# An attention stage of one core whose sparse blocks run in another order, large beside small, with the local blocks between them

## What is computed

```python
# sparse: per block of 128 queries, the 256 best keys by an indexer, 8 heads, one key/value head
score = jnp.where(causal[None], score, -jnp.inf)
_, sel = lax.top_k(score, topk)
logits = jnp.einsum('bqhd,bqkd->bhqk', qb, kg) * scale + bias
logits = jnp.where(valid[:, None], logits, -jnp.inf)
p = jax.nn.softmax(logits, axis=-1)
...
# local: window of 128, 8 query heads, 2 key/value heads, a learned sink per head
logits = jnp.where(mask, logits + bias, -jnp.inf)
m = jnp.maximum(jnp.max(logits, axis=-1, keepdims=True), sink)
p = jnp.exp(logits - m) / (jnp.sum(jnp.exp(logits - m), axis=-1, keepdims=True) + jnp.exp(sink - m))
```

## Time and profile before

| | before |
|---|---|
| three executions, us | 3624.54, 3630.03, 3897.19 |
| median, us | 3630.03 |
| the profiled execution, us | 3625.67 |
| its span in the profile, us | 3623.6 |
| TensorE busy, of the span | 3391.3 us (94%) |
| VectorE / ScalarE / GpSimd busy | 69% / 46% / 19% |

### The profile page before, as it was taken

How to read it: one execution, slowest core, us unless ns; L and a number is a source line. 1 busy time by engine, 2 the same in 40 slices (tenths; PEclk the granted TensorE clock), 3 DMA queues, 4 the chain that set the end, 5 groups by cost and what they waited for, 6 DMA issues and landing times.

```text
span 3623.6 us, 40448 instructions
## 1 busy us (share of the span) xinstructions
PE 3391.3 (94%) x15020; PEld 2697.7 (74%) x15064; DVE 2506.4 (69%) x4097; ACT 1661.5 (46%) x2030; POOL 677.7 (19%) x370
## 2 busy tenths in 40 slices
PE   7999999968888999969899999999999999999997
PEld 5788778855556666647777888888888888888886
DVE  5899999987776766536555765567566766576566
ACT  5767888126566666663222333333333333333332
POOL 1012132334455656650000000000000000000001
PEclk9999999979999999989999999999999999999998
DMA  6322233352211120027554432223332332223230
GB/s 168 50 90 94 93 105 103 117 158 72 52 51 40 43 59 24 17 66 213 174 163 117 151 128 93 92 83 128 122 105 93 108 128 92 97 102 112 92 105 32
DMA packets 232927, 356.36 MB, mean 98 GB/s; under 512 B 43421, under 2 KB 150573, under 8 KB 218782
## 3 DMA queue, kind: packets, MB, share of 16 engines
q1 hardware_dynamic: 231678, 349.42, 31.2%
q0 software_dynamic: 1056, 4.36, 0.3%
HBM read 289.60 MB, written 64.13 MB: 98 GB/s over the span
## 4 chain that ended last, share of the span: by engine, by line
PE 50%; DVE 2%; ACT 1%; DMA 1%; issue 1%; POOL 0%; SPq 0%; DVEq 0%
PE tl_ps L88 17%; PE tl_ps L89 17%; PE tl_ps L90 17%; DMA tl_pr<-in_w_pb_dram 0%; DVE tl_stat L1449 0%; PE tl_ps L1643 0%; DVE tl_sg L1439 0%; ACT tl_ph L1330 0%; DMA tl_yr<-yt 0%; DVE tl_xr L1459 0%; DVE tl_xr L1466 0%; DVE tl_nmr L1538 0%; ACT tl_woh L1350 0%; ACT tl_sg L1332 0%; DVE tl_xr L1467 0%
## 5 line engine op out<-in xcount | busy, mean ns | idle before, releaser
L90 PE MATMUL tl_ps<-tl_xh,tl_ul 128*128 128x512 f32 x1536 | 597.5, 389 | 0.0
L88 PE MATMUL tl_ps<-tl_xh,tl_uh 128*128 128x512 f32 x1536 | 597.5, 389 | 0.0
L89 PE MATMUL tl_ps<-tl_xl,tl_uh 128*128 128x512 f32 x1536 | 597.5, 389 | 0.0
L1378 ACT ACTIVATE tl_c<-tl_ps,tl_cb,tl_cw 128x512 f32<-128x512 f32 x192 | 148.8, 777 | 748.5 <-PE tl_ps L90 748.5
L789 POOL TENSOR_TENSOR plo<-pf,phi 128x1024 fp32r<-128x1024 f32 x168 | 415.7, 2476 | 345.1 <-ACT phi L838 344.9
L88 PE MATMUL frt_acc<-frt_xh,frt_wh 128*128 128x512 f32 x864 | 339.2, 393 | 18.7 <-issue 8.7
L89 PE MATMUL frt_acc<-frt_xl,frt_wh 128*128 128x512 f32 x864 | 338.1, 391 | 0.0
L90 PE MATMUL frt_acc<-frt_xh,frt_wl 128*128 128x512 f32 x864 | 337.8, 391 | 0.0
L88 PEld LDWEIGHTS tl_ps<-tl_xh,tl_uh 128*128 128x128 f32 x1536 | 288.3, 188 | 60.0
L90 PEld LDWEIGHTS tl_ps<-tl_xh,tl_ul 128*128 128x128 f32 x1536 | 288.3, 188 | 59.9
L89 PEld LDWEIGHTS tl_ps<-tl_xl,tl_uh 128*128 128x128 f32 x1536 | 288.3, 188 | 59.6
(11 more groups left out here) (270 smaller groups left out, 7460.1 us busy)
## 6 DMA issues: line engine op xcount, KB each, us to landing
tl_ur<-in_w_up_dram SPq DMA_DIRECT2D x96, 1024.0 KB, 4.8
tl_dr<-in_w_down_dram SPq DMA_DIRECT2D x64, 768.0 KB, 4.4
zt<-frt_out SPq DMA_DIRECT2D x108, 256.0 KB, 4.6
frt_wr<-in_w_main_dram SPq DMA_DIRECT2D x51, 512.0 KB, 4.2
att_raw<-zt SPq DMA_DIRECT2D x64, 256.0 KB, 4.1
tl_sg<-zt SPq DMA_DIRECT2D x64, 256.0 KB, 4.5
frt_xr<-in_xt_dram SPq DMA_DIRECT2D x12, 1024.0 KB, 7.5
yt<-y SPq DMA_DIRECT2D x32, 256.0 KB, 2.3
```

The source lines that it names most:

```text
L88: pe.matmul(out, ahi, bhi, start=first, stop=False)
L89: pe.matmul(out, ahi, blo, start=False, stop=False)
L90: return pe.matmul(out, alo, bhi, start=False, stop=last)
L1378: act.activation(c[:, k % 2, a, :], up(k, a), ACT.Identity, scale=cw[:, 2, a, k % NS:k % NS + 1], bias=cb[:, a, k % NS:k % NS + 1]).then_i ...
```

## The change

Five things. `seq` is now taken from a list; "w" is the next local block, a number a sparse one. As before all engines follow the plan that the same code makes out of it.

```diff
-        seq = [(kind, n) for n in range(NB) for kind in range(2)]
+        order = "1 3 6 9 w 0 12 w w 15 w w 14 w w 13 w 2 11 w w 10 w 4 w 8 w 5 w w 7 w".split()
+        near_blocks = iter(range(NB))
+        seq = [(1, next(near_blocks)) if o == "w" else (0, int(o)) for o in order]
+        masked = [n for kind, n in seq if not kind and n >= 2]
...
-        mx = s.sb("mx", [P, HEADS, NCH], F32)
-        mm8 = s.sb("mm8", [P, HEADS], F32)
+        mx = s.sb("mx", [P, 2, HEADS, NCH], F32)
+        mm8 = s.sb("mm8", [P, 2, HEADS], F32)
...
+            if op == "top" and b >= 2 and b - 2 not in peaked:
+                return False
...
-                    if n >= 5:
-                        sp.wait_ge(S["std"], first[index[0, n - 3] + 1])
-                    sp.dma_start(msk[:, n % 3, 0:(n + 1) * P], mask[n, :, 0:(n + 1) * P]).then_inc(S[f"lm{n % 3}"], 16)
+                    i = masked.index(n)
+                    if i >= 3:
+                        sp.wait_ge(S["std"], first[index[0, masked[i - 3]] + 1])
+                    sp.dma_start(msk[:, i % 3, 0:(n + 1) * P], mask[n, :, 0:(n + 1) * P]).then_inc(S[f"lm{i % 3}"], 16)
...
             load_queries(0)
             sp.dma_start(snk[:], sinks.rearrange("(o h) -> o h", o=1).broadcast_to([P, HEADS])).then_inc(S["lsn"], 16)
+            load_queries(1)
             sp.wait_ge(S["c1"], 2)
-            load_queries(1)
+            load_near(0)
+            load_near(1)
             for op, b, x in plan:
                 if op == "q" and b + 2 < len(seq):
                     load_queries(b + 2)
+                elif op == "vt" and seq[b][1] + 2 < NB:
+                    load_near(seq[b][1] + 2)
```

More of the change, by code:

```diff
@@ L728, in load_queries, with load_near @@
                 if not kind and n >= 2:
-                    if n >= 5:
-                        sp.wait_ge(S["std"], first[index[0, n - 3] + 1])
-                    sp.dma_start(msk[:, n % 3, 0:(n + 1) * P], mask[n, :, 0:(n + 1) * P]).then_inc(S[f"lm{n % 3}"], 16)
[L732 to L741, removed]
+                    i = masked.index(n)
+                    if i >= 3:
+                        sp.wait_ge(S["std"], first[index[0, masked[i - 3]] + 1])
+                    sp.dma_start(msk[:, i % 3, 0:(n + 1) * P], mask[n, :, 0:(n + 1) * P]).then_inc(S[f"lm{i % 3}"], 16)
+            def load_near(n):
+                if n >= 2:
+                    sp.wait_ge(S["kd"], n - 1)
+                    sp.wait_ge(S["vt"], n - 1)
+                t0 = n * P
+                for v in range(2):
+                    for half in range(2):
+                        sp.dma_start(kbr[half * DH:(half + 1) * DH, n % 2, v, :, v:P],
+                                     zt[C_KB:C_KB + P, t0 + v:t0 + P].rearrange("(g d) t -> d g t", g=2)).then_inc(S[f"lb{n % 2}"], 16)
+                    sp.dma_start(vbr[:, n % 2, v, v:P], zt[C_VB:C_VB + P, t0 + v:t0 + P]).then_inc(S[f"lb{n % 2}"], 16)
             load_queries(0)
             sp.dma_start(snk[:], sinks.rearrange("(o h) -> o h", o=1).broadcast_to([P, HEADS])).then_inc(S["lsn"], 16)
+            load_queries(1)
             sp.wait_ge(S["c1"], 2)
-            load_queries(1)
+            load_near(0)
+            load_near(1)
             for op, b, x in plan:
@@ L921, in top @@
                     w = P * min(2, n + 1)
-                    dve.tensor_reduce(mm8[:, h:h + 2], sq[:, k, :].rearrange("p (a b) -> p a b", a=2)[:, :, 0:w],
+                    dve.tensor_reduce(mm8[:, b % 2, h:h + 2], sq[:, k, :].rearrange("p (a b) -> p a b", a=2)[:, :, 0:w],
                                       AX.X, ALU.max).then_inc(S["sqr"], 1)
@@ L926, in top @@
                 if n >= 2:
-                    dve.wait_ge(S[f"lm{n % 3}"], 16 * ((n - 2) // 3 + 1))
-                    m = msk[:, n % 3, c * CH:c * CH + w]
+                    r = masked.index(n)
+                    dve.wait_ge(S[f"lm{r % 3}"], 16 * (r // 3 + 1))
+                    m = msk[:, r % 3, c * CH:c * CH + w]
                 else:
@@ L933, in top @@
                 dve.tensor_tensor_reduce(junk[:, i % 2, 0:w], sq[:, k, 0:w], m, 1.0, 4 * NEG, ALU.add, ALU.max,
-                                         mx[:, h, c:c + 1]).then_inc(S["sqr"], 1)
+                                         mx[:, b % 2, h, c:c + 1]).then_inc(S["sqr"], 1)
             def negmax(b):
@@ L939, in negmax @@
                 if kind:
-                    link(dve.tensor_tensor(mm8[:], mm8[:], snk[:], ALU.max))
+                    link(dve.tensor_tensor(mm8[:, b % 2], mm8[:, b % 2], snk[:], ALU.max))
                 else:
-                    link(dve.tensor_reduce(mm8[:], mx[:, :, 0:-(-(n + 1) * P // CH)], AX.X, ALU.max))
+                    link(dve.tensor_reduce(mm8[:, b % 2], mx[:, b % 2, :, 0:-(-(n + 1) * P // CH)], AX.X, ALU.max))
                 if b:
@@ L946, in negmax @@
                                   nid[:].rearrange("p (o q) -> p o q", o=1).broadcast_to([P, HEADS, P]),
-                                  mm8[:].rearrange("p (h o) -> p h o", o=1).broadcast_to([P, HEADS, P]),
+                                  mm8[:, b % 2].rearrange("p (h o) -> p h o", o=1).broadcast_to([P, HEADS, P]),
                                   ALU.mult).then_inc(S["dgd"], 1)
@@ L1063, in logits @@
                     if n >= 2:
-                        m = msk[:, n % 3, i * P:(i + 1) * P]
+                        m = msk[:, masked.index(n) % 3, i * P:(i + 1) * P]
                     elif near == 0:
```

## The result

The changed kernel takes 3636.3 us (median of 19 runs, 3632.5 to 3639.9), the kernel before 3630.0 (19 runs beside them, of which 3897 and 4319 stand far apart and are left out of the ratio): ratio 1.0021, interval 1.0014 to 1.0028. Slower by 0.2%, where 0.6% faster was forecast and the range ended at 3636. In the profiled executions the spans are 3633.8 and 3623.6 us, and the 10 us lie in the attention stage: it ends at 1613.7 instead of 1603.2 us, what stands ahead of it and behind it keeps its length. The profiled execution of the kernel before lies 4 us under its median, that of the changed kernel at its median, so some 6 to 8 of the 10 us are the difference of the kernels.

What follows compares the result with a forecast made beforehand. The prediction took TensorE, held in the attention stage by VectorE's reductions and fixed work per block, as the bound. From the profiled 3625.7 us, 18 less for levelling and 1 more for stores gave 3609, range 3587 to 3636.

Steps and rivals of the forecast that it cites:

- Need and bound: Attention stage: TensorE needs 648 of 803 us in both orders; only the 155 us loss can change.
- The line from VectorE's work to the loss: Attention stage: loss read off VectorE's work per stretch; 29 us less by twenty steps, 8 by ten, 18 taken.
- The eighteen stretches of ten steps: Attention stage between first and last ten steps: losses sorted by VectorE work, 133 us before, 125 after.
- The prices of VectorE: Attention stage: fixed times per VectorE operation, such as queries 1.69 and diagonal 1.45 us, summed per twenty steps.
- The clock: Attention stage behind step 140: a fall to 0.95 would cost 8 us more; left out of the sum.
- Given back at the end: Steps 150 to 183: blocks ending there with three gaps in the logits lose 20 + 8 + 3 = 31 us.
- The slow rival: Last 43 steps: short blocks lose some 60 us instead of 31, giving 3647 us; decides from about 49; chance 0.1.
- the rival of no gain: Attention stage: loss goes by block ends and gaps, as many as before; 3619 to 3632 us, chance 0.25.
- Start: Start of the attention stage: first row maxima of other blocks cost between nothing and 2 us more.
- Buffers, masks, loads: Attention stage: two row-maxima buffers give nothing by themselves; masks and local loads taken as nothing, bound 3 us once.
- Stores: Evictions waiting for the store of two blocks before: 0 to 8 us, 1 us taken.
- What would show it: Signs: first 80 steps lose about 59 us, TensorE idle a tenth behind the start, reduction waits about 30 us.

Runs made afterwards that it cites:

- e5: Changed kernel with GpSimd's subtraction replaced by clears that read nothing from SBUF (low parts of the probabilities left out): 3617.5 us, ratio 0.9972 to the kernel before.
- e6: Changed kernel with the old order of blocks and GpSimd's subtraction replaced by clears that read nothing: 3626.5 us, ratio 0.9992 to the kernel before.
- e1: Changed kernel with the old order of blocks, all other edits kept: 3629.6 us, ratio 0.9995 to the kernel before.
- e10: Changed kernel with the diagonal's product written as eight multiplications by a scalar of each partition: 3716.4 us, ratio 1.0238 to the kernel before.
- e4: Changed kernel with four added matmuls of 512 columns in each of the 15 steps without logits: 3638.0 us, ratio 1.0020 to the kernel before.

## Why the prediction was wrong, by its steps

- **Need and bound**: the count of instructions and the reading that only the loss of this stage could change were right (the plans have 25 places without logits, not 26); so was the reading that VectorE's reductions, evictions and block ends hold TensorE.
- **The line from VectorE's work to the loss** is the step that failed. On twenty steps it gave 47 us less in the first 80 and 18 more behind them; it came to 26 less and 37 more. The eighteen stretches of ten steps came to 143 us, not to 125. The line was fitted to before, where VectorE's work and the smallness of blocks fell together; work alone did not carry the loss over. Stretches from 40, 140 and 160 on show it: forecast 11, 20, 8, measured 20, 26, 15, with the clock at 0.91, 0.89 and 0.98.
- **The prices of VectorE** The earlier trace rows hid the term of the sign. The queries' 1.69 and the diagonal's 1.45 us are 1.22 each plus a stand behind GpSimd, and the sum took it to cost the same wherever it falls. Without GpSimd's reads the new order is 7 us faster than the old (e5, e6), the forecast's side at well under half its size; with them the stand, and what follows from it, costs 18 us in the new and about 1 in the old. The difference, 17 us give or take 6, is the larger part of the 27 us by which the sum was off.
- **The clock** was left out of the sum as neutral. The early stretches pay as before ((1 - clock) x length, 11.6 us for steps 20 to 79 against 11.8), the last three 13.7 against 1.7. The 8 us more that the prediction named beside the Trainium skill's rule, and left out, had sign and place right. Half-clock matmuls say 9 us; it overlaps with the stand, since e5 had 46 of them instead of 91.
- **Given back at the end**: the 31 us forecast are 20 + 8 + 3 of the stretches from step 140 on, which lost 46, against 18 before; behind step 150 it is 42 against 12. The slow rival named this place; its point of decision, 49 us, was not reached, and it was enough to be slower all the same, since the gain ahead was smaller than forecast. The time, 3636, lies between that rival's 3647 and the 3632 at which the rival of no gain ended.
- **Start**: it loses 2 us more, at its bound (34 against 32). **Buffers, masks, loads**: nothing, as said (e1). **Stores**: 0.5 us of VectorE in one place, ScalarE none; right.
- **What would show it**: TensorE idle for a tenth of steps 20 to 79 came true (10.6, 11.1, 11.0%), and the waits on reductions fell to 34 of the forecast 30. But the loss there was 46 us and not 32: idle shows neither the clock nor broken overlap.

Not settled is how the clock, the stand and the order's own waits share the 10 us between the kernels: they change each other, and no run holds one fixed.

## What to carry to other kernels

Before a mean of VectorE's rows goes into a sum, look at its shortest and longest: a row that takes twice its shortest may be a wait inside the instruction, here for GpSimd, and what it cost depended on where it fell: the sums were equal, 35 and 34 us, and the price was not. A schedule that puts short blocks together needs a look at its gaps one by one, with the clock behind each; levelling the sum of an engine's work is not enough. Don't split an operation that contends with another engine into many small ones without looking at what runs beside it: here it cost 80 and 55 us.

## What the runs showed of the hardware

- VectorE's operation on two tensors in SBUF waits inside its row for a running GpSimd operation, however small it is (128x8: 1.97 us instead of 0.17), and GpSimd's waits likewise (3.32 instead of 2.34). VectorE loses 34 of 508 us to it. GpSimd's clears do hardly the same: with them the diagonal's mean is 1.25 us. A multiplication of 128x128 by a scalar of each partition waits too, 0.28 us alone and up to 2.47 (e10), though a reciprocal of 128x128, one tensor in SBUF as well, never does (0.88 to 0.96 us). Whether the multiplication's scalar makes it one of two inputs or it runs in one of the two-port modes that the Trainium skill's page (above) names, no run tells.
- Extra matmuls in idle steps hold the clock up: with 13.7 us of them the kernel's own took some 12 us less of TensorE's time (e4), and the execution was as long as without.
